# High and low halves in one 512-column matmul in two convolution layers of a six-layer block

## What is computed

```python
def short_conv_mixer(xn, w_in, conv_w, conv_b, w_out):
    """y = W_out( B * conv3(C * h) * silu(z) ), causal depthwise width-3 conv."""
    bg, cg, hv, z = jnp.split(xn @ w_in, 4, axis=-1)
    u = cg * hv
    y = lax.conv_general_dilated(
        u, conv_w[:, None, :].astype(u.dtype), window_strides=(1,),
        padding=[(CONV_WIDTH - 1, 0)], dimension_numbers=("NWC", "WIO", "NWC"),
        feature_group_count=A_WIDTH) + conv_b
    return (bg * y * jax.nn.silu(z)) @ w_out
```

## Time and profile before

| | us |
|---|---|
| median of 3 runs | 938.21 |
| lowest, highest | 937.90, 944.13 |
| profiled execution | 939.07 |
| its span, first to last instruction | 937.4 |
| TensorE busy in the span | 901.0 |
| VectorE, ScalarE, GpSimd busy | 650.4, 493.8, 311.8 |
| looped units of the first layer | 39.18 to 108.5 |
| looped units of the second layer | 450.49 to 519.87 |

### The profile page before, as it was taken

The page is one execution under the profiler, slowest core; times in us unless marked ns, Lnnn a source line. Parts: engine busy times, 40 slices in busy tenths (PEclk is TensorE's granted clock), DMA queues, the critical chain, the costliest instruction groups (busy, mean ns, idle before and its releaser), DMA issues.

```text
span 937.4 us, 16800 instructions
## 1 busy us (share of the span) xinstructions
PE 901.0 (96%) x6761; PEld 847.6 (90%) x6761; DVE 650.4 (69%) x1019; ACT 493.8 (53%) x716; POOL 311.8 (33%) x263
## 2 busy tenths in 40 slices
PE   6999999999989998989999999999999999999996
PEld 5999997788879987779999999999999998989996
DVE  5787666889894788975876676877646644656642
ACT  5544445664775659755444453353535336586632
POOL 8543322473132243223433227774103000223310
PEclk9999999999999999999999999999999999999999
DMA  9796436344314443346684535445673652425411
GB/s 251 202 237 188 180 104 239 119 145 171 134 60 150 141 143 122 122 115 168 164 227 183 180 135 180 135 150 189 209 263 129 239 181 91 168 102 180 159 45 45
DMA packets 123585, 148.70 MB, mean 159 GB/s; under 512 B 9561, under 2 KB 79102, under 8 KB 123518
## 3 DMA queue, kind: packets, MB, share of 16 engines
q1 hardware_dynamic: 121472, 145.63, 48.3%
q10 hardware_dynamic: 1582, 1.12, 0.4%
q0 software_dynamic: 464, 1.02, 0.3%
HBM read 146.70 MB, written 1.05 MB: 158 GB/s over the span
## 4 chain that ended last, share of the span: by engine, by line
PE 62%; DVE 11%; ACT 3%; issue 1%; POOL 1%; DMA 1%; SPq 0%; ACTq 0%; POOLq 0%; DVEq 0%
PE acc L1739 44%; PE aux L1739 17%; DVE wlo L916 4%; DVE wlo L935 1%; DMA raw<-in_pool_w_in 1%; ACT whi L483 1%; DVE work L1250 1%; DVE work L1261 1%; POOL sqy L1653 1%; PE aux L2100 1%; DVE arena L1020 0%; DVE sqy L1110 0%; DVE hf L1120 0%; ACT arena L739 0%; ACT work L715 0%
## 5 line engine op out<-in xcount | busy, mean ns | idle before, releaser
L916 DVE TENSOR_TENSOR wlo<-raw,whi 128x2048 fp32r<-128x2048 f32 (+5 forms) x114 | 273.9, 2428 | 90.8 <-ACT whi L483 89.1
L1739 PE MATMUL acc<-xh,whi 128*128 128x256 f32 x1128 | 322.2, 286 | 4.0 <-DVE wlo L916 2.7
L1739 PE MATMUL acc<-xl,whi 128*128 128x256 f32 x1128 | 319.5, 283 | 0.0
L1739 PE MATMUL acc<-xh,wlo 128*128 128x256 f32 x1128 | 319.4, 283 | 0.0
L483 ACT ACTIVATE whi<-raw 128x2048 fp32r<-128x2048 f32 (+5 forms) x115 | 197.6, 1745 | 77.7 <-PE acc L1739 36.7
L1739 PEld LDWEIGHTS acc<-xh,whi 128*128 128x128 f32 x1128 | 216.4, 192 | 6.2 <-issue 4.9
L1739 PEld LDWEIGHTS acc<-xl,whi 128*128 128x128 f32 x1128 | 216.4, 192 | 0.0
L1739 PEld LDWEIGHTS acc<-xh,wlo 128*128 128x128 f32 x1128 | 216.3, 192 | 0.0
L1662 POOL CAST yh<-ytmp 128x256 fp32r<-128x256 f32 x24 | 25.2, 1051 | 206.1 <-DVE ytmp L1501 119.1
L1739 PE MATMUL aux<-yh,whi 128*128 128x256 f32 x288 | 82.3, 286 | 2.0 <-DVE stat L1254 2.0
L1739 PE MATMUL acc<-whi,xh 128*128 128x512 f32 (+1 forms) x208 | 81.4, 392 | 1.6 <-DVE arena L1020 0.5
(11 more groups left out here) (340 smaller groups left out, 1719.0 us busy)
## 6 DMA issues: line engine op xcount, KB each, us to landing
raw<-in_a_w_in SPq DMA_DIRECT2D x52, 512.0 KB, 6.7
raw<-in_sb_w_in SPq DMA_DIRECT2D x48, 512.0 KB, 5.6
raw<-in_b_w_in SPq DMA_DIRECT2D x36, 512.0 KB, 5.5
raw<-in_pool_w_in SPq DMA_DIRECT2D x32, 512.0 KB, 5.7
raw<-in_a_w_out SPq DMA_DIRECT2D x16, 512.0 KB, 4.9
raw<-in_pool_w_out SPq DMA_DIRECT2D x16, 512.0 KB, 5.5
raw<-in_sb_w_out SPq DMA_DIRECT2D x16, 512.0 KB, 5.2
raw<-in_b_w_out SPq DMA_DIRECT2D x8, 512.0 KB, 5.1
```

The lines of the kernel that those rows point to most:

```text
L916: TT(wlo[b][:, lo:hi], (raw_third if third else raw[b])[:, lo:hi], whi[b][:, lo:hi].bitcast(F32), ALU.subtract).then_inc(lo_ready, 1)
L1739: return nc.tensor.matmul(out_, lhsT, rhs, start=start, stop=stop, skip_group_check=True)
```

## The change

It touches the input projection of the two convolution layers, units 2 to 7; units 0 and 1 and the output projection are as before.

- `xh` and `xl` become the two halves of one tensor `xhl` of 16 tiles; `xhl[:, kt::8, :]` is `xh[:, kt]` and `xl[:, kt]`.
- TensorE takes the column tiles one behind the other, in the order `PARTS` = (0, 1, 3, 2), that is B, C, z, h; for each it goes over all kt. For each kt one matmul of `whi` by 512 columns writes a whole bank (high product in columns 0 to 255, low in 256 to 511), and one of `wlo` by `xh`, 256 columns, is added to the low half. Tile n has bank n for itself, and all four banks belong to every unit. So each bank waits until it was emptied of the unit before (`part_free`).
- A tile in PSUM is now two numbers. ScalarE copies the low half to SBUF (`low`, four a unit), VectorE adds the high half from PSUM to it (`add_high`, four a unit, each followed by a wait for its own end), and only then come the products with r and `cgS`, now from SBUF: seven instructions where there were three. ScalarE's copy of C for `cgS` goes, except in units 0 and 1.
- On VectorE the second half of `wlo` of unit j+1 now stands between the adds of tiles 1 and 2 of unit j, and its first half behind the taps of unit j-1; so the halves are made for the next unit, where before they were for the one after it. On ScalarE the two halves of `whi` of unit j+1 stand in front of the copies of unit j.
- The loops on TensorE, ScalarE and VectorE are written out.

```diff
--- before.py
+++ after.py
@@ -118,7 +118,8 @@
 
         xT = put("xT", [P, NK, T])
         xh_at = base[0]
-        xh, xl = put("xh", [P, NK, T], F32R), put("xl", [P, NK, T], F32R)
+        xhl = put("xhl", [P, 2 * NK, T], F32R)
+        xh, xl = xhl[:, 0:NK, :], xhl[:, NK:2 * NK, :]
         yh_at = base[0]
         yh, yl = put("yh", [P, NK, T], F32R), put("yl", [P, NK, T], F32R)
         sqx = at("sqx", [P, 2 * NK, T], F32, xh_at)
@@ -325,6 +326,7 @@
         MLA_SPLITS = {0: ((C0 + 7, 2), (C0 + 7, 3)), **quarters(C0 + 8, (2, 3)), **quarters(C0 + 9, (5, 6))}
         SPARSE_TANH = {0: (24,), 1: (26,), 4: (28,), 5: (30,)}
         MLA_TANH = {1: (40,), 2: (42,), 4: (44,), 5: (46,)}
+        PARTS = (0, 1, 3, 2)
         FILLERS = (("v", 1), ("z", 1), ("z", 2), ("v", 2), ("z", 3), ("v", 3))
         FILL = [(f, 4 * half, 4) for f in range(6) for half in range(2)]
         FILLED = (2, 4, 6, 8, 10, 12)
@@ -533,28 +535,57 @@
             y_count = [0]
 
             def conv_layer(u0, m):
-                cgS, zr, sz, yA = (arena[:, n, :] for n in (10, 12, 14, 17))
-
-                def step(b, i, j, u):
-
-                    act.wait_ge(unit_done, u + 1)
-                    A(cgS, acc_tile(b, 1), ACT.Copy).then_inc(sem("cg_ready"), 1)
-                    act.wait_ge(landed[b], i * 64 + 64 * (u0 // 2 + 1))
-                    third = isinstance(u, int) and u == A0
-                    split_half(b, 0, SLOT // 2, third)
+                cgS, u0t, zr, bgr, sz, yA = (arena[:, n, :] for n in (10, 11, 12, 13, 14, 17))
+
+                def copy_c(j):
+                    act.wait_ge(unit_done, u0 + j + 1)
+                    A(cgS, acc_tile(j, 1), ACT.Copy).then_inc(sem("cg_ready"), 1)
+
+                def silu_z(j):
                     act.wait_ge(sem("zr_ready"), ky + j + 1)
                     A(sz, zr, ACT.Silu).then_inc(sem("sz_ready"), 1)
-                    split_half(b, SLOT // 2, SLOT, third)
+
+                def high(j):
                     act.wait_ge(sem("y_ready"), y0 + j + 1)
-                    A(yh[:, ds(j, 1), :], yA, ACT.Copy).then_inc(sem("yh_ready"), 1)
+                    A(yh[:, j, :], yA, ACT.Copy).then_inc(sem("yh_ready"), 1)
+
+                def low(j, i, dst, used):
+
+                    if i < 3:
+                        act.wait_ge(sem("part_psum"), 18 * (ky // 8) + 3 * (j - 2) + i + 1)
+                    else:
+                        act.wait_ge(unit_done, u0 + j + 1)
+                    act.wait_ge(sem(used), ky + j)
+                    A(dst, acc[:, PARTS[i], T:2 * T], ACT.Copy).then_inc(sem("part_low"), 1)
 
                 y0 = y_count[0]
                 ky = 0 if m == 0 else 8
-                for b in range(2):
-                    step(b, 0, b, u0 + b)
-                with act.Fori(1, 4) as i:
-                    for b in range(2):
-                        step(b, i, i * 2 + b, i * 2 + (u0 + b))
+                copy_c(0)
+                act.wait_ge(landed[0], 64 * (u0 // 2 + 1))
+                split_half(0, 0, SLOT // 2, m == 0)
+                silu_z(0)
+                split_half(0, SLOT // 2, SLOT, m == 0)
+                high(0)
+                copy_c(1)
+                split(u0 + 3, (0,))
+                silu_z(1)
+                split(u0 + 3, (1,))
+                high(1)
+                low(2, 0, bgr, "gate_ready")
+                low(2, 1, cgS, "u0_ready")
+                low(2, 2, zr, "sz_ready")
+                silu_z(2)
+                low(2, 3, u0t, "u_ready")
+                for j in range(3, 8):
+                    split(u0 + j + 1)
+                    low(j, 0, bgr, "gate_ready")
+                    low(j, 1, cgS, "u0_ready")
+                    high(j - 1)
+                    low(j, 2, zr, "sz_ready")
+                    silu_z(j)
+                    low(j, 3, u0t, "u_ready")
+                split(u0 + 9)
+                high(7)
                 y_count[0] += 8
                 split(u0 + 10)
 
@@ -1040,31 +1071,59 @@
                 def col(n, j):
                     return G[:, ds(j + n, 1)]
 
-                def step(b, j, u):
-                    dve.wait_ge(unit_done, u + 1)
-                    TT(zr, acc_tile(b, 3), r[:, :], ALU.mult).then_inc(sem("zr_ready"), 1)
-                    dve.wait_ge(sem("cg_ready"), j + (8 * k + 1))
-                    TT(u0t, cgS, acc_tile(b, 2), ALU.mult).then_inc(sem("u0_ready"), 1)
-                    TT(bgr, acc_tile(b, 0), r[:, :], ALU.mult).then_inc(sem("acc_free"), 1)
-                    dve.wait_ge(hi_ready, u * 2 + 5)
-                    third = isinstance(u, int) and u == A0
-                    split_half(b, 0, SLOT // 2, third)
-                    dve.wait_ge(sem("u_ready"), j + (8 * k + 1))
+                def evict(j):
+                    dve.wait_ge(unit_done, u0 + j + 1)
+                    TT(zr, acc_tile(j, 3), r[:, :], ALU.mult).then_inc(sem("zr_ready"), 1)
+                    dve.wait_ge(sem("cg_ready"), 2 * k + j + 1)
+                    TT(u0t, cgS, acc_tile(j, 2), ALU.mult).then_inc(sem("u0_ready"), 1)
+                    TT(bgr, acc_tile(j, 0), r[:, :], ALU.mult).then_inc(sem("acc_free"), 1)
+
+                def add_high(j, i, dst):
+
+                    n = 24 * k + 4 * (j - 2) + i + 1
+                    dve.wait_ge(sem("part_low"), n)
+                    TT(dst, acc[:, PARTS[i], 0:T], dst, ALU.add).then_inc(sem("part_free"), 1)
+                    dve.wait_ge(sem("part_free"), n)
+
+                def taps(j):
+                    dve.wait_ge(sem("u_ready"), 8 * k + j + 1)
                     me.link(TS(c1, upad[:, 2:T + 2], col(w0 + 16, j), col(G_CB + 8 * j2, j), ALU.mult, ALU.add))
                     me.link(STT(c1, upad[:, 1:T + 1], col(w0 + 8, j), c1, ALU.mult, ALU.add))
                     me.link(STT(c1, upad[:, 0:T], col(w0, j), c1, ALU.mult, ALU.add))
-                    dve.wait_ge(hi_ready, u * 2 + 6)
-                    split_half(b, SLOT // 2, SLOT, third)
-                    dve.wait_ge(sem("gate_ready"), j + (8 * k + 1))
+
+                def gated(j):
+                    dve.wait_ge(sem("gate_ready"), 8 * k + j + 1)
                     TT(yA, c1, g, ALU.mult).then_inc(sem("y_ready"), 1)
 
-                for b in range(2):
-                    step(b, b, u0 + b)
-                with dve.Fori(1, 4) as i:
-                    me.enter(i, 1, 6)
-                    for b in range(2):
-                        step(b, i * 2 + b, i * 2 + (u0 + b))
-                me.leave(3)
+                def low(u, half, third=False):
+                    dve.wait_ge(hi_ready, 2 * u + 1 + half)
+                    split_half(u % 2, SLOT // 2 * half, SLOT // 2 * half + SLOT // 2, third)
+
+                evict(0)
+                low(u0 + 2, 0, k == 0)
+                taps(0)
+                low(u0 + 2, 1, k == 0)
+                gated(0)
+                evict(1)
+                low(u0 + 3, 0)
+                taps(1)
+                for j in range(2, 8):
+                    if j > 2:
+                        taps(j - 1)
+                        low(u0 + j + 1, 0)
+                    gated(j - 1)
+                    add_high(j, 0, bgr)
+                    TT(bgr, bgr, r[:, :], ALU.mult).then_inc(sem("acc_free"), 1)
+                    add_high(j, 1, cgS)
+                    low(u0 + j + 1, 1)
+                    add_high(j, 2, zr)
+                    TT(zr, zr, r[:, :], ALU.mult).then_inc(sem("zr_ready"), 1)
+                    add_high(j, 3, u0t)
+                    TT(u0t, cgS, u0t, ALU.mult).then_inc(sem("u0_ready"), 1)
+                taps(7)
+                low(u0 + 9, 0)
+                gated(7)
+                low(u0 + 9, 1)
 
             conv_layer(A0, 0, 0)
             split(A0 + 10)
@@ -1860,19 +1919,22 @@
             def conv_layer(u0, m, k, y0):
                 unit(u0, in_tiles(0), xh, xl, x_wait(m))
                 unit(u0 + 1, in_tiles(1), xh, xl, spread_late(m))
-                whv, wlv = zip(*(w_view(b, 8, 512) for b in range(2)))
-                with pe.Fori(1, 4) as i:
-                    for b in range(2):
-
-                        pe.wait_ge(sem("acc_free"), i * 2 + (8 * k + b - 1))
+                for j in range(2, 8):
+                    u = u0 + j
+                    wh, wl = w_view(u, 8, 512)
+                    for i, n in enumerate(PARTS):
+
+                        if j == 2:
+                            pe.wait_ge(sem("acc_free"), 8 * k + (1 if i < 2 else 2))
+                        else:
+                            pe.wait_ge(sem("part_free"), 24 * k + 4 * (j - 3) + i + 1)
+                        c = slice(P * n, P * n + P)
                         for kt in range(8):
-                            if kt in (0, 4):
-                                pe.wait_ge(lo_ready, i * 4 + (2 * (u0 + b) + 1 + kt // 4))
-                            for n in range(4):
-                                ins = three(acc_tile(b, n), whv[b][:, kt, P * n:P * n + P],
```

(8 more changed lines are left out.)

## The result

The changed kernel takes 944.85 us (median of 5 runs, 943.95 to 949.0) where the kernel before takes 938.21 in the same runs: ratio 1.0074, 95% interval 1.0052 to 1.0096. It is slower by 0.5 to 1.0%, within the range given and on the side forecast; 946.0 was predicted. The profiled execution took 944.85 us with a span of 943.2, against 939.07 and 937.4.

What follows compares the result with a forecast made beforehand. TensorE was taken to bound the kernel, but to wait for VectorE after the change: +3.88 us a layer, +7.8 in sum, 939.07 to 946.9 profiled, which lies 0.86 above the median, so 946.0 us; range 940 to 952.

Steps and rivals of the forecast that it cites:

- TensorE's stream: Units 2 to 7: a pair costs 0.3466 us instead of 0.36, a unit 11.09 instead of 11.52; at most 5.1 us won.
- rival D: On TensorE, a 512 costs 0.24 us, so no shorter stream; 946.0 us, counted within the forecast's chance of 0.55.
- The stop in unit 2: TensorE waits in unit 2 of each layer for the second half of `wlo`; stall 2.66 us.
- H(3): Time when unit 3's second half of `wlo` is ready: 466.27, where TensorE would want it at 465.63.
- The loop on VectorE: Distance between second halves of successive units on VectorE: 11.28 us, plus 0.36 for the GpSimd lock, 11.64.
- Rival A: The VectorE/GpSimd lock doesn't bite: loop 11.28 us, last output unit +1.5 us a layer, 941.2 us; chance 0.2.
- Rival B: More semaphore waiting in VectorE's loop: 0.6 us a cycle, +6 us, 952 us; chance 0.17 together with Rival E.
- The tail: Layer's end: `yl(7)` lies under the last `wlo` half, ends 0.6 us after it, and the last output unit waits.
- The sum of a layer: The last output unit of each convolution layer starts at 535.27 instead of 531.39 (second layer's numbers): +3.88 us.
- Rival E: TensorE's clock falls in the 2.66 us stop; small chance, in Rival B's range, 0.17 for both.
- L: Theory set up for the experiments: VectorE's work order binds, first in units 0 and 1, then its loop; TensorE's stops only show it.
- Rival C: VectorE keeps up, loop under 11.09 us, TensorE binds after unit 3: +0.8 us a layer, 939.8 us; chance 0.08.

Runs made afterwards that it cites:

- the reordered loop: Changed kernel with only VectorE's order changed: unit 2's second `wlo` half before the taps, in the loop both halves moved to where VectorE waited; 946.32 us.
- The last kernels: On top of the reordered loop, TensorE takes kt 0 to 3 first and the layer start is reordered; 937.08 us, with two 256s for the 512 939.86.
- the halves side by side: Changed kernel with `xh` and `xl` of one kt adjacent in SBUF, so the 512 moving columns are one run; 945.28 us, ratio 1.0083.

## Why the prediction held, and where it was off

- **TensorE's stream**: 5.1 us to win at most, by 0.2266 us for a 512. It was so in part of the stretches only (pair 0.3467); in others the pair took 0.3535, half of the saving: rival D in part. As forecast it hardly counted here.
- **The stop in unit 2**: predicted 2.66 us late; the matmul starts at 458.37, 2.65 after the one before it, which is about 2.5 late, of which 2.37 is recorded as idle.
- **H(3)**: predicted 15.78 us after the start of unit 2; TensorE takes the half up at 470.12 - 454.35 = 15.77. It comes 0.35 late there and not 0.64 (0.19 of it recorded as idle), since unit 2 itself ran at the slower pace (0.2 us) and its first matmul after the stop took 0.1 more.
- **The loop on VectorE**: sum 11.28, plus 0.36 for GpSimd's lock, 11.64. Measured 11.34. The sum of the rows was right to 0.06; the step that failed is the term for the lock, 0.36 where 0.09 is seen: "`yl` begins under the scaling, which ends 1.22 after `gated`, so it ends at 1.96". `yl` doesn't wait there. It began 0.27 us after the scaling, a multiplication of two SBUF tiles (478.25), and took what it takes alone, and only the `wlo` behind (479.05 above) was longer, 2.38 for 2.29:

```profile
478.52 0.75 POOL L1628 TENSOR_TENSOR yl<-arena,yh 128x256 f32 x1 [4.50 <-ACT yh L550]
```

  The term took the recorded durations for the time of the lock. The next instruction of VectorE starts 0.34 after the scaling, at 478.59, so `yl` and the scaling share 0.15 us by the recorded durations and at most 0.07 by the starts. The Trainium skill (SBUF — State Buffer, SBUF: two separate sides) has the lock held for the whole instruction. For the long `wlo` the trace agrees (the tail, next); for an overlap as short as this one it doesn't decide. Rival A was right for the loop and wrong for the tail, and its +1.5 us a layer is too little. Rival B, more waiting, didn't come: it names 0.6 us a cycle above the sum of the rows, and 0.06 came.
- **The tail**: there the lock bit as predicted. `yl(7)` began under the last `wlo` (534.55 to 536.84), took 2.14 instead of 0.75 and ended 0.58 after it (0.6 was predicted), and the last output unit waited 0.58 us for it:

```profile
535.28 2.14 POOL L1628 TENSOR_TENSOR yl<-arena,yh 128x256 f32 x1 [4.50 <-ACT yh L550]
```

- **The sum of a layer**: +3.88 predicted, +2.48 measured; five cycles, to H(8), at 0.30 too much are 1.5 us and account for the 1.4. For two layers that is 2.8 too many; the 1.12 late start, which is not the change's, and -0.3 elsewhere made the profiled time 944.85 where 946.9 was summed. So part of the closeness, 946.0 against 944.85, is luck: the layers alone would give 4.96 us, not 6.6.
- **Rival E**: it happened, in the first layer alone, and cost nothing there. After the same stop of 2.37 us the granted clock was down to 0.50, the level of 1.2 GHz, for about 3 us:

```profile
44.00:45.00 1.00, 0.69 (x2) 0.59 (x3) 0.93 (x3) 0.37 (x2) 0.00 (x0) 0.72 0.00 0
45.00:47.00 2.00, 2.00 (x9) 1.71 (x8) 0.75 (x2) 2.00 (x3) 1.43 (x2) 0.50 0.43 119
47.00:48.00 1.00, 1.00 (x5) 0.86 (x5) 0.85 (x1) 1.00 (x3) 0.43 (x1) 0.58 1.14 344
```

  Unit 2 lost about 1.4 us by it, and unit 3 then had no stop. Both layers come out at 83.22: it lay in the time in which TensorE would have waited for VectorE anyway. This is a second sign for L. The prediction had set a small chance on it, from the one stop of 2.06 us that left the clock alone; in other traces it didn't (below).
- **Rival C**, that even a VectorE that keeps up wins nothing since the stop of unit 2 eats it, held in this order of TensorE: the reordered loop gave 946.32, more than the 939.8 that C names, as it brought a second stop. The last kernels show that the stop is a matter of order, and what is left when it goes is a gain of 1.0 us.
- The rest of the forecast was borne out by what it said would show it: the releasers of TensorE's stops were `wlo` and `yl` only, never `whi` or the banks, and idle on VectorE was before the add of tile 3 and before the taps.

Why single executions of one kernel differ by up to 5 us (943.95 to 949.0) can in part be read off, since the same unchanged stages stand in twelve traces. From the last output unit of the second layer to the last matmul it is 395.9 to 396.0 us in five of them; 397.4 to 397.5 in five more, which have one stretch of about 3 us at a granted clock of 0.50; 398.0 in the kernel before, with the stop of 2.06 us and no such stretch; and 399.5 in the kernel with the halves side by side, which has both. So the one costs 1.5 us and the other 2.1. The stop is in one trace with the change and in one without it; the low stretch in this part is in six of the ten with it and in neither of the two without. Add a stop of 1.3 us for a `wlo` near 220 us in three traces, and up to 1.1 at the start of unit 2, and the sum passes 5 us.

The median of the changed kernel is 6.6 us above the kernel before and its layers account for 5.0. The rest is not traced, but the mean granted clock of the executions points to it: 0.992 in four of five of the changed kernel, 0.996 or more in 50 of the 51 of the kernel before that were run beside the experiments. Why the changed kernel falls to the low clock more often was not tried. Not settled either is what sets the pair at 0.3467 or 0.3535.

## What to carry to other kernels

When a loop order on TensorE is turned round, ask of each operand and each bank how long after the unit's start it is now needed: going tile by tile took 4.4 us of grace from the second half of the weights, and in the kernel before that alone cost as much as the whole change. In the changed kernel it was not the only cause: VectorE's chain, through units 0 and 1 and its fuller loop of 11.34 us, holds the last output unit back as long even when the first stop is shorter. Neither the loop nor TensorE's order put right alone, nor both together without the start of the layer, brought the median below 944. A stop on the busiest engine is where a late chain shows; find the engine with no slack (add work to it and see whether the time moves one for one) before removing the stop, or the next one takes its place. The saving of 2 to 4% on TensorE's stream in these units was only had when the orders of all the engines that feed it were made anew; it came to 2.8 us from the merging and 1.0 net.

## What the hardware showed that was not expected

- Matmuls of 512 and 256 columns in turn run at one of two paces, 0.3467 or 0.3535 us a pair, at a granted clock of 1.00 in both, and keep it until the next stop or late start; in the streams of 256 alone that were counted each took 0.1200.
- After a stop of 2.4 us on TensorE the granted clock was 0.50 for about 3 us in one layer and not in the other of the same execution. Stops of 1.90 us (586.64 in the changed kernel) and of 2.06 us (622.95 with the halves side by side) were followed by it in some traces and not in others. Where TensorE binds, one such stretch cost 1.5 us.
- A VectorE product of two SBUF tiles of 256 columns, recorded as 0.42 us, did not visibly delay a GpSimd instruction that started 0.27 us into it (0.07 us before VectorE's next start), while under a `wlo` of 2048 columns one of 0.75 us took 2.14.
